# Two transformer blocks on one core: the modulation matrix laid out with its outputs on partitions and summed along rows by VectorE

## The reference

```
mod = silu(c) @ ada_w[l] + ada_b[l]            # [6 * 1024]; ada_w[l] is [1024, 6144]
shift, scale, gate = three sections of 1024, for this sub-layer
h = rms_norm(x, norm_g[l, 2*part]) * (1 + scale) + shift
x = x + gate * rms_norm(attention_or_ffn(h), norm_g[l, 2*part + 1])
```

## Time and profile before

| | before |
|---|---|
| median of 3 runs | 1045.24 us (1043.79 to 1045.63) |
| profiled execution, its own time | 1045.63 us |
| its span, first to last instruction | 1044.3 us |
| TensorE busy | 1015.4 us (97%) |
| VectorE busy | 693.1 us (66%) |
| ScalarE busy | 491.2 us (47%) |
| GpSimd busy | 37.9 us (4%) |
| moved by DMA | 225.12 MB |
| mean granted TensorE clock | 0.984 of full |

### The profile page before, as it was taken

One profiled execution on the slowest core, in us unless ns is written; L12 is line 12 of the kernel. 1 busy time (PEld: TensorE's weight loads), 2 busy tenths in 40 slices (PEclk: granted clock), 3 DMA queues, 4 the chain that ended last, 5 costly groups with the idle time before them and its releaser, 6 DMA issues.

```text
span 1044.3 us, 16304 instructions
## 1 busy us (share of the span) xinstructions
PE 1015.4 (97%) x6958; PEld 932.5 (89%) x6958; DVE 693.1 (66%) x832; ACT 491.2 (47%) x688; POOL 37.9 (4%) x55
## 2 busy tenths in 40 slices
PE   5999999999999999999989999999999989999998
PEld 4988999899998998899889999997998879999997
DVE  5756656777756776787676556566998685445453
ACT  6644433553333435555464434335665573443441
POOL 2000000010000000100010000001000100000000
PEclk9999999989999999999989999999999999999999
DMA  9843567548866785596537666664666327554501
GB/s 374 353 162 120 185 250 262 193 144 330 317 240 238 268 300 202 184 351 251 202 116 268 220 228 235 224 240 145 275 251 242 121 79 255 191 193 171 202 1 41
DMA packets 32744, 225.12 MB, mean 216 GB/s; under 512 B 3885, under 2 KB 4245, under 8 KB 6176
## 3 DMA queue, kind: packets, MB, share of 16 engines
q1 hardware_dynamic: 30960, 219.53, 57.8%
q0 software_dynamic: 1424, 4.31, 1.2%
q10 hardware_dynamic: 288, 0.24, 0.1%
HBM read 223.00 MB, written 1.06 MB: 215 GB/s over the span
## 4 chain that ended last, share of the span: by engine, by line
PE 93%; DVE 4%; ACT 2%; issue 1%; DMA 1%; POOL 0%; SPq 0%; DVEq 0%
PE psum L596 20%; PE psum L597 19%; PE psum L598 19%; PE psum L624 9%; PE psum L625 9%; PE psum L626 9%; PE psum L780 2%; ACT work_v L332 1%; DVE work L349 1%; PE psum L846 1%; PE psum L301 1%; DVE low L518 1%; DMA x_res<-in_x 1%; DVE x_res L414 1%; PE psum L464 0%
## 5 line engine op out<-in xcount | busy, mean ns | idle before, releaser
L518 DVE TENSOR_TENSOR low<-raw,high 128x2048 fp32r<-128x2048 f32 (+1 forms) x160 | 363.2, 2275 | 185.4 <-ACT high L510 185.4
L596 PE MATMUL psum<-h_hi,high 128*128 128x256 f32 x1600 | 459.8, 287 | 2.0 <-DVE h_lo L328 1.5
L597 PE MATMUL psum<-h_lo,high 128*128 128x256 f32 x1600 | 455.9, 285 | 0.0
L598 PE MATMUL psum<-h_hi,low 128*128 128x256 f32 x1600 | 455.6, 285 | 0.0
L510 ACT ACTIVATE high<-raw 128x2048 fp32r<-128x2048 f32 (+1 forms) x160 | 302.5, 1900 | 76.4 <-PE psum L626 64.3
L596 PEld LDWEIGHTS psum<-h_hi,high 128*128 128x128 f32 x1600 | 310.3, 194 | 8.4 <-issue 5.5
L597 PEld LDWEIGHTS psum<-h_lo,high 128*128 128x128 f32 x1600 | 310.4, 194 | 1.3 <-issue 0.2
L598 PEld LDWEIGHTS psum<-h_hi,low 128*128 128x128 f32 x1600 | 310.2, 194 | 0.0
L624 PE MATMUL psum<-high,y_hi 128*128 128x512 f32 x328 | 128.7, 392 | 0.5 <-DVE y_lo L868 0.5
L625 PE MATMUL psum<-low,y_hi 128*128 128x512 f32 x328 | 128.0, 390 | 0.0
L626 PE MATMUL psum<-high,y_lo 128*128 128x512 f32 x328 | 127.7, 389 | 0.0
(11 more groups left out here) (155 smaller groups left out, 791.2 us busy)
## 6 DMA issues: line engine op xcount, KB each, us to landing
raw<-in_gate_up SPq DMA_DIRECT2D x66, 1024.0 KB, 5.0
raw<-in_ada SPq DMA_DIRECT2D x48, 1024.0 KB, 5.5
raw<-in_down SPq DMA_DIRECT2D x33, 1024.0 KB, 5.2
raw<-in_mix SPq DMA_DIRECT2D x14, 1024.0 KB, 5.0
raw<-in_moba_qk SPq DMA_DIRECT2D x8, 1024.0 KB, 5.2
raw<-in_diff_qk SPq DMA_DIRECT2D x8, 1024.0 KB, 6.0
raw<-in_qk SPq DMA_DIRECT2D x4, 1024.0 KB, 13.9
raw<-in_branch SPq DMA_DIRECT2D x4, 1024.0 KB, 5.0
```

What stands on the lines that cost most here:

```text
L518: nc.vector.tensor_tensor(low[n % N_LO][:, s], raw[i % N_RAW][:, s], high[n % N_HI][:, s].bitcast(F32), ALU.subtract).then_inc(*rest.up(key))
L596: nc.tensor.matmul(to, a, hi(k), start=first, stop=False)
L597: nc.tensor.matmul(to, a, lo(k), start=False, stop=False)
L598: m = nc.tensor.matmul(to, r, hi(k), start=False, stop=last and j > j0)
```

## The change

The matrix is laid out the other way round: partitions are now outputs. An ada slab holds 2 x 128 outputs with all 1024 of their inputs each, so a section is complete after four slabs. `silu(c)` stands in every partition (`c_row`, 128 x 1024, loaded with a broadcast by GpSimd), and VectorE multiplies a slab's half by it and sums along the row in one instruction, two to a slab, straight into a column of `mod_raw`. The section's bias and norm weight come from one loaded tile, `mod_given`. There is nothing left to be summed over partitions, so the matmuls of lines 457 and 464, the tile `ada`, its clearing and its bias loads are gone. The gate, which is needed along the free axis, is written from its column form to memory and read back with a broadcast by GpSimd (`pool_gain`).

```diff
-        def pe_modulation(block, halves, spare=()):
...
-                        m = nc.tensor.matmul(o[:, k:k + 1], a, ones[:, 0:1], start=True, stop=True)
...
-                        nc.tensor.matmul(o[:, :], ones, a, start=True, stop=True).then_inc(
...
+        def dve_modulation(layer, part, what):
+
+            key, a = (layer, part, what), mod_section(layer, part, what)
+            o, b = mod_raw[:, a:a + KC], mod_given[:, a:a + KC]
+            yield from dve.wait_ge(mod_in, "given")
+            yield from dve.wait_ge(summed, ("section", key))
+            place = mod_cols[:, 4 * layer + 2 * part + 1 - what, :] if what < 2 else gain_col[:, 2 * layer + part, :]
+            if what == 0:
+                nc.vector.tensor_tensor(place, o, b, ALU.add).then_inc(*modulated.up(key))
+                return
+            nc.vector.scalar_tensor_tensor(out=o, in0=o, scalar=2.0 - what, in1=b, op0=ALU.add, op1=ALU.add).then_inc(
+                *summed.up(("biased", key)))
+            yield from dve.wait_ge(summed, ("biased", key))
+            g = MOD_GAIN[key]
+            nc.vector.tensor_tensor(place, o, mod_given[:, g:g + KC], ALU.mult).then_inc(*modulated.up(key))
+
+        def pool_gain(layer, part, stage):
+
+            n, slot = 2 * layer + part, GAIN_SLOT[layer, part]
+            yield from pool.wait_ge(modulated, (layer, part, 2))
+            column = bass.AP(gain_dram.tensor, n * D, [[1, P], [P, KC]])
+            nc.gpsimd.dma_start(column, gain_col[:, n, :], allow_slow_non_contiguous=True).then_inc(*gain_out[n].up("column", by=16))
+            yield from pool.wait_ge(gain_out[n], "column")
+            if stage is not None:
+                yield from pool.wait_ge(gained, (stage, 1, 1))
+            nc.gpsimd.dma_start(gain[slot][:, :], gain_dram[n].partition_broadcast(P)).then_inc(
+                *gain_in[slot].up((layer, part), by=16))
...
         def dve_sum(i, m):
-            block, k = divmod(m, KC)
+            raw_rows = raw[i % N_RAW][:, :].rearrange("p (a n) -> p a n", a=2)
             yield from dve.wait_ge(raw_in[i % N_RAW], i)
...
-            nc.vector.scalar_tensor_tensor(
-                out=ada[:, :], in0=raw[i % N_RAW][:, :], scalar=c_act[:, k:k + 1], in1=ada[:, :],
-                op0=ALU.mult, op1=ALU.add).then_inc(*summed.up((block, k)))
...
+                last = nc.vector.tensor_tensor_reduce(
+                    out=w, in0=w, in1=c_row[:, :], scale=1.0, scalar=0.0, op0=ALU.mult, op1=ALU.add,
+                    accum_out=mod_raw[:, 2 * m + a:2 * m + a + 1])
...
         def scalar():
...
-            nc.scalar.activation(c_act[:, :], col("c"), ACT.Silu).then_inc(*small_act.up("c"))
...
             yield from act_values("v1", 0)
+            yield from act.wait_ge(c_in, "c")
+            nc.scalar.activation(c_row[:, :], c_row[:, :], ACT.Silu).then_inc(*small_act.up("c"))
```

More of the change, by code:

```diff
@@ L36 @@
 COLUMNS = {}
-for _name, _n in (("mix_pre", KC), ("ffn_pre", KC), ("c", KC), ("g00", KC), ("g02", KC), ("g10", KC), ("g12", KC),
-                  ("conv", 3 * AC), ("subln", 1), ("b_f", NT * H), ("lam", 4 * DIFF)):
+for _name, _n in (("mix_pre", KC), ("ffn_pre", KC), ("conv", 3 * AC), ("subln", 1), ("b_f", NT * H), ("lam", 4 * DIFF)):
     COLUMNS[_name] = (sum(w for _, w in COLUMNS.values()), _n)
 N_COLUMNS = sum(w for _, w in COLUMNS.values())
+N_MOD = 12 * KC
+MOD_GAIN = {(layer, part, what): N_MOD + KC * (4 * layer + 2 * part + (what == 2))
+            for layer in range(2) for part in range(2) for what in (1, 2)}
 IDENT, FLIP, TRI, ONES = 0, P, 2 * P, 3 * P
@@ L98, in load_order @@
         order += [("main", m)] + [("ada", n) for n in after.get(m, [])]
-    return order, [late for _, _, late in plan]
-STREAM, AT_NORM = load_order()
+    return order
+STREAM = load_order()
 def moving_order(blocks):
@@ L366, in pe_post_norm @@
             yield from pe_turn(stage, 0)
-            for block, halves in LATE_BLOCK[stage]:
-                yield from pe_modulation(block, halves, [5, 7] if stage == 1 else [4, 5, 6])
             if stage != 1:
@@ L433, in dve_post_norm @@
                         yield from dve_split_h(stage, 0, 4, 8)
-            for block, halves in LATE_BLOCK[stage]:
-                yield from dve_modulation(block, halves)
         def pool_post_norm(stage):
@@ L467, in dve_modulation @@
-        def dve_modulation(block, halves):
-            for half, layer, part, what in sections_of(block, halves):
-                if what < 2:
-                    key = layer, part, what
-                    yield from dve.wait_ge(gathered, key)
-                    place, o = mod_cols[:, 4 * layer + 2 * part + 1 - what, :], psum[bank_of["mod", *key]][:, 0:KC]
-                    if what == 0:
-                        m = nc.vector.tensor_copy(place, o)
-                    else:
-                        m = nc.vector.scalar_tensor_tensor(out=place, in0=o, scalar=1.0, in1=col(f"g{layer}{2 * part}"),
-                                                           op0=ALU.add, op1=ALU.mult)
-                    m.then_inc(*modulated.up(key))
-                else:
-                    slot = GAIN_SLOT[layer, part]
-                    for c in range(2):
-                        key = ("gain", (layer, part), c)
-                        yield from dve.wait_ge(gathered, key)
-                        yield from dve.wait_ge(gain_in[slot], (layer, part))
-                        g = gain[slot][:, c * 512:(c + 1) * 512]
-                        nc.vector.tensor_tensor(g, psum[bank_of[key]][:, :], g, ALU.mult).then_inc(*modulated.up(key))
@@ L489, in build_program, with mod_section @@
-        pe_due, dve_due = [], []
-        def come_due(due, m):
-            block, k = divmod(m, KC)
-            if k == KC - 1 and (block == 5 or not AT_NORM[block]):
-                due.append((block, (0,) if block == 5 else (0, 1)))
+        def mod_section(layer, part, what):
+            return KC * (6 * layer + 3 * part + what)
+        def dve_modulation(layer, part, what):
[12 more added lines that the diff above has]
+            nc.vector.tensor_tensor(place, o, mod_given[:, g:g + KC], ALU.mult).then_inc(*modulated.up(key))
@@ L599, in pe_still, with pe_moving @@
             m.then_inc(*slab.up(n, (name, index), *alias))
-            yield from pe_slab_done()
-        def pe_moving(name, parts, data, ready, kcs, k_all, freed, tag, between={}, hold=0):
+        def pe_moving(name, parts, data, ready, kcs, k_all, freed, tag, between={}):
             hi, lo = data
@@ L1529, in gpsimd @@
             yield from pool_post_norm(4)
+            yield from pool_gain(1, 1, 2)
             yield from pool_post_norm(5)
@@ L1607 @@
         "down2": np.concatenate([slabs(a["ffn_w_out_2"][i], 2, D) for i in range(2)]),
-        "ada": np.concatenate([slabs(a["ada_w_2"][i], 1, SLAB) for i in range(2)]),
-        "ada_b": a["ada_b_2"].reshape(-1, SLAB),
-        "mix_post": a["norm_mix_post"], "ffn_post": a["norm_ffn_post"], "norm_g": a["norm_g_2"],
+        "ada": np.concatenate([put(w.T.reshape(-1, 2, P, D).transpose(0, 2, 1, 3)).reshape(-1, P, SLAB) for w in a["ada_w_2"]]),
+        "c": a["c_2"][0],
+        "mod_given": np.concatenate([columns(a["ada_b_2"].reshape(-1)), columns(a["norm_g_2"].reshape(-1))], axis=1),
+        "mix_post": a["norm_mix_post"], "ffn_post": a["norm_ffn_post"],
     }
```

131 lines of the change are left out of this document (41 added, 90 removed).

## The result

The kernel after takes 1032.2 us, the median of 4 runs (1031.19 to 1032.68), against 1045.19 us (1043.79 to 1045.63) before on the same chip: ratio 0.9878, 95% interval 0.9867 to 0.989. It is 13.0 us faster; 8.7 had been forecast from the profiled execution, and 1036.9 us is 4.7 too much. The profiled execution of after has a span of 1030.4 us, 13.9 less than that of before.

A forecast was written before the change was run, and what follows sets the result against it. TensorE, on 93% of the chain of waits, was taken as the bound. Terms 3.4 + 0.8 + 1.2 + 1.9 + 1.3 + 0.4 - 0.3 - 0.2 + 0.2 = 8.7 us took 1045.6 to 1036.9 us, range 1032.8 to 1040.8.

The forecast's parts named there:

- start: Four L349 at the start no longer stretched by the clear: 0.8 us gained, bounds 0.6 to 1.2.
- block 1 in the first FFN: Modulation matmuls between two weight slabs, with nothing to hide them, go away: 3.4 us gained.
- stage 0: Cast L326 no longer stretched by the clear, so TensorE continues earlier: 1.2 us gained, bounds 0.7 to 1.5.
- stage 1: Without L464 the first L624 comes 2.6 us earlier at half clock: 0.4 us gained, between -0.35 and 1.3.
- stage 2: Two L349 that TensorE's turn waits for, no longer stretched by the clear: 1.9 us gained, bounds 1.05 to 2.1.
- stage 3 and `diff` attention: Two L349 without the clear gain 1.3 us; dearer slab sums on VectorE around `diff` attention lose 0.2.
- output projection of `diff`: Half block's bare matmuls go, but VectorE's copy is late next: 0.2 us gained instead of 1.84.
- stage 4: No clear here; without L464 in the hole the second turn may run at half clock: 0.3 us lost.
- the rival on the clock: Larger holes keep stages at 1.2 GHz longer, 1.65 us lost each, to 1041 us; chance 0.11. Could also fall out otherwise.
- The column DMA: Issue of the gate's 1024 pieces of 4 bytes may touch VectorE in stage 3: 0.3 us kept back; landing free.
- The matmuls in the holes: Between turns in stages 0, 2, 3 and 4 TensorE waits anyway; removing them makes the hole larger, not shorter.
- the silu: ScalarE's 128 x 1024 silu, up to 2.35 us late, hidden by 2.4 us slack before TensorE near 50 us: cost 0.

The follow-up runs named there:

- bare_fill: fill plus stand-ins for the modulation's matmuls only inside the first FFN and ahead of the `diff` output projection; 1032.01 us, 4.6 more than fill.
- bare_back: Kernel after with stand-ins for the modulation's matmuls only inside the first FFN and ahead of the `diff` output projection; 1035.82 us.
- clear_back: Kernel after with four GpSimd memsets of the old clears' size put back at the start and in stages 0, 2 and 3; 1038.1 us.
- clears_fill: clear_back with idle matmuls over `c_row` between the turns of each stage; 1034.51 us, 7.1 more than fill.
- late_clear: Kernel before with each GpSimd clear of `ada` but block 2's held until the second tile is split; 1035.43 us, ratio 0.9911.
- after_again: Kernel after, unchanged, executed once more for a second trace; 1030.48 us, span 1028.9.
- fill_late_column: fill with the gate's column DMA held until the second tile is split, in stages 1, 3 and 4; 1030.64 us.
- norm_matmuls_2: Kernel after with stand-ins for the modulation's matmuls only between the two turns of each norm, second timing; 1030.63 us.
- matmuls_back: Kernel after with unused stand-ins for the modulation's matmuls at all their old places, holes and bare places; 1033.92 us.
- fill: Kernel after with idle matmuls in TensorE's hole between the two turns of stages 0 to 4; 1027.37 us, ratio 0.9834.

## Why the prediction was wrong

The direction was right, and the terms of the start, of block 1 and of stages 2 and 4 agree with the table; the sum was 4.7 us short. By the terms, in gains (the second pair of traces, the repeats, in brackets):

| term | forecast | measured |
|---|---|---|
| start | 0.8 | 0.7 (0.7) |
| block 1 in the first FFN | 3.4 | 3.5 by bare_fill and bare_back |
| stage 0 | 1.2 | 3.7 (2.5) |
| stage 1 | 0.4 | 0.7 (2.6) |
| stage 2 | 1.9 | 2.0 (1.9) |
| stage 3 and `diff` attention | 1.3 - 0.2 | 2.5 (2.4) |
| output projection of `diff` | 0.2 | 0.9 to 1.0 |
| stage 4 | -0.3 | -0.2 (-0.2) |

Stage 0 is what the segment of 7.2 (6.0) leaves after the 3.5 of block 1, the row of stage 3 what 3.4 (3.3) leaves after 0.9. The 2.6 of stage 1 in the repeats, where neither trace has half clock there, are 0.8 us up to the turn of tile 1, the 1.2 us that TensorE waited in it for VectorE's gain (L486, which is gone after), and 0.6 behind it. The start's 0.7 is no more than what two executions of one kernel differ by there, and the clear put back at the start cost 0.1 and 0.3 us by stage 0 (clear_back, clears_fill): that it agrees with the forecast may be luck.

**The clears of stages 0 and 3, the step that failed.** The prediction took the stretch at half clock as given: "if the clock rises at the same moment as before, only half of the shift is won", so that the whole shift was the upper bound (1.5 and 1.6 us). In fact the clear's hole also kept the clock low. One clear costs 1.5 us of wait (clear_back, and clears_fill with full clock), as the rows had it for stages 0 and 3 (1.46 and 1.6; in stage 2, where the old clear came later beside the pair, 2.1); where it also brings 3.4 us more at half clock, 0.4 to 0.9 us come on top, and 1.9 to 2.4 us were measured for one clear in stages 0 and 3 (clear_back, clears_fill, late_clear). The half clock of stage 0 went from 10.2 to 3.4 us (6.8 in the repeat), that of stage 3 from 6.8 to 3.4. The prediction did write that it could fall out the other way in stage 0, in the rival on the clock, but gave this no size in the sum. Together these stages are 2.6 of the 4.7 us by the repeats, and 3.9 by the first pair; of the latter 1.0 is the stretch that after has in stage 1 and after_again in stage 0, and so luck of the execution.

**The `diff` output projection, 0.2 against 0.9.** The step that VectorE would be late next was right, but the copy was not what the chain before hung on. In the timelines of after, VectorE and then TensorE:

```profile
810.87 0.68 DVE L967 COPY work<-psum 128x512 f32<-128x512 f32 x1
...
816.55 0.74 PE L986 MATMUL psum<-const,work 128*128 128x128 f32 x4 [0.23 <-DVE work L978]
817.77 0.80 PE L986 MATMUL psum<-const,work 128*128 128x128 f32 x4 [0.48 <-DVE work L978]
```

Before, the transposes that follow this copy (L1021, now L986) began at 831.11 us right behind TensorE's own matmuls, with no wait for VectorE. They came as late as TensorE was, and only behind them did it wait 0.47 us. Now the transposes wait 0.23 and 0.48 us for VectorE. From the last matmul ahead of them to the first behind them it is 2.62 us, before it was 1.79. So of 1.7 us of matmuls 0.8 came back there and 0.9 to 1.0 was won. The prediction priced the removal by VectorE's shift alone (824.49 to 824.3).

**The column DMA.** The 0.3 us in stage 3 was right as a duration (1.19 instead of 0.88 us). The Trainium skill, page "SBUF — State Buffer", section "Who interferes with whom", says that whoever issues first holds the shared ports for the whole instruction, and names for DMAs with descriptors from GpSimd only that these are held up by VectorE. Here GpSimd's L467 began first (715.79 against 715.87 us), and VectorE was lengthened beside it and not without it, which agrees with the first. But L1504's issue in the earlier trace rows began first too and lengthened nothing, so the order alone doesn't tell when it happens. fill_late_column shows that with the clock held the 0.31 us is off the path. With the clock as it is in after, no run shows what it costs.

**The matmuls in the holes.** "Taking them away makes the hole larger, not shorter", thus costs nothing: almost. They had kept some of the clock, and without them 1.4 to 1.9 us are lost (norm_matmuls_2). The sum had 0.3 for that in stage 4 and 0.9 in stage 1. This loss is inside the measured rows above. It is the rival "the clock takes it back", and it is real, but smaller than the clock that the clears gave back.

**The rest.** Block 1, stage 2 and stage 4 came out as worked out; stage 4's second turn takes 1.94 us, as the prediction had it. In stage 2 a clear alone is worth less than the table's 2.0: its segment lost 1.1 in clear_back and 1.5 in clears_fill. The new sum was 1218 ns where 1.22 us was read off L797. `ck_lo` (L1325) begins at 48.19 us and ends at 48.60, 1.8 us ahead of the latest end that the prediction allowed, and TensorE shows no wait for it, so the silu costs nothing.

In sum, the change splits thus: without the clears 9.2 us (late_clear), the rest, from late_clear to after, 3.2. Of this the matmuls are 1.7 (matmuls_back): 3.3 at the bare places (4.6 with the clock held), less what they kept of the clock in the holes. The other 1.5 us lie neither in the clears nor in the matmuls. The spans of late_clear and matmuls_back differ by 1.2 us, of which 0.3 lie between stages 0 and 1, 0.4 between stages 3 and 4 and 0.4 behind stage 4; no run takes them apart.

## What to carry to other kernels

Where a wait on a TensorE-bound path ends in a stretch at half clock, price the wait and the clock apart: shortening the wait can also shorten the stretch, and filling a hole with idle matmuls can remove it (4.8 us here, for five lines). Before work is taken out of a hole, ask what it did for the clock, and look for memsets on GpSimd beside the instruction that the hole ends on; moving them cost nothing here and was some 70% of this change's gain. When TensorE work is removed, check for the next waits on both engines, not for the one that moves. And ask where small transfers land: beside bulk loads, one of 4 KB was worth 3.3 us.

## What the runs showed of the hardware

- A GpSimd memset of 128x2048 fp32 (1.80 us) beside two VectorE scalings of 128x512 fp32 makes them last 2.38 instead of 0.88 us (clear_back, stage 2), and 0.88 again when it is moved away (late_clear).
- The same kernel does not have the same stretches at half clock in each execution: one of 3.4 us moved from stage 1 to stage 0 between two traces of after, and the segments moved by 1.6 and 1.0 us.
- 23.9 us at half clock cost 4.8 us by the medians and 2.7 to 4.2 by the profiled spans, 0.1 to 0.2 us for each, not 0.5 (fill against after).
- With one-column and 512-column fp32 matmuls in the holes the time at half clock was 17.1 and 20.5 us instead of 23.9, with the 512-column ones of fill none. bare_back has 20.5 us as well, with nothing in the holes, so 3.4 us more or less are no proof.
- A column of 1024 pieces of 4 bytes lands in 9.8 us (median of four, in after) and, while it was under way beside the weight loads, all DMAs together moved 22 to 29 GB/s over 6 us, against 369 and 232 right behind it (fill, fill_late_column).
